# Three changes of order in a hybrid attention block: residual tiles turned back before the last one is turned forth, eight PSUM banks in the last down projection, outputs scaled ahead of the query products

## The reference

```python
def rms_norm(x, gain):
    y = xf * lax.rsqrt(jnp.mean(xf * xf, axis=-1, keepdims=True) + NORM_EPS) * gain
...
    # chunk_gated_delta_rule, one step a chunk
    def step(state, inp):
        v_new = u_i - w_i @ state
        o_i = q_i @ state + qk_i @ v_new
        state = state * gt_i + k_i.T @ v_new
...
    o = o * lax.rsqrt(jnp.mean(o * o, axis=-1, keepdims=True) + NORM_EPS) * head_norm * silu(z)
    y = sigmoid(g_a) * o + sigmoid(g_b) * multiscale_causal_pool(...)
    mixer = y @ w_out
...
    h = h + hybrid_mixer(rms_norm(h, norm_mix), ...)
    h = h + conv_gated_mlp(rms_norm(h, norm_ffn), w_up, conv_ffn, w_down)
    return rms_norm(h, norm_final)[:, N_META:]
```

## Time and profile before

| what | us |
| --- | --- |
| median of 3 runs (1780.7 to 1784.41) | 1781.15 |
| the profiled execution | 1779.33 |
| its span | 1777.5 |
| TensorE busy | 1692.4 |
| VectorE busy | 909.4 |
| ScalarE busy | 609.4 |
| GpSimd busy | 472.9 |
| mean granted clock of TensorE | 0.98 |

### The profile page before, as it was taken

One profiled execution on the slowest core, in us unless ns is written; L12 is line 12 of the kernel. 1 busy time (PEld: TensorE's weight loads), 2 busy tenths in 40 slices (PEclk: granted clock), 3 DMA queues, 4 the chain that ended last, 5 costly groups with the idle time before them and its releaser, 6 DMA issues.

```text
span 1777.5 us, 30704 instructions
## 1 busy us (share of the span) xinstructions
PE 1692.4 (95%) x12131; PEld 1616.4 (91%) x12131; DVE 909.4 (51%) x971; ACT 609.4 (34%) x984; POOL 472.9 (27%) x469
## 2 busy tenths in 40 slices
PE   6999999986999999999879999999999999999997
PEld 6999999986999999999879898989989989989986
DVE  5565644582445454454450656455455455455457
ACT  6334465443434444343322531211211212212213
POOL 3221212124343444434202121221221221221220
PEclk9999999997999999999979999999999999999998
DMA  5223443336353544545584111111111111111112
GB/s 187 75 91 109 135 131 92 110 88 185 110 151 100 156 107 136 151 119 142 132 257 150 36 36 36 59 47 35 59 47 35 58 42 42 47 47 47 47 35 95
DMA packets 239653, 167.41 MB, mean 94 GB/s; under 512 B 43880, under 2 KB 225991, under 8 KB 238456
## 3 DMA queue, kind: packets, MB, share of 16 engines
q1 hardware_dynamic: 205492, 130.39, 25.7%
q10 hardware_dynamic: 33892, 36.28, 6.0%
q0 software_dynamic: 224, 0.12, 0.0%
HBM read 124.40 MB, written 42.37 MB: 94 GB/s over the span
## 4 chain that ended last, share of the span: by engine, by line
PE 84%; DVE 7%; DMA 2%; ACT 2%; SPq 1%; issue 1%; DVEq 1%; ACTq 0%; POOL 0%; POOLq 0%
PE gb L787 60%; PE db L1115 13%; PE db L926 4%; DMA yb_d<-ybs 1%; PE db L840 1%; PE db L991 1%; DVEq L1550 1%; PE db L992 1%; SPq L583 1%; DMA yo<-ot_d 1%; DVE cacc L1587 1%; DVE tiny L1748 1%; DVE vb L1751 1%; DVE hx L1879 1%; PE db L1068 1%
## 5 line engine op out<-in xcount | busy, mean ns | idle before, releaser
L787 PE MATMUL gb<-u_hi,w_hi 128*128 128x342 f32 (+2 forms) x2520 | 824.3, 327 | 14.7 <-ACT ht L1459 5.1
L787 PE MATMUL gb<-u_lo,w_hi 128*128 128x342 f32 (+2 forms) x2520 | 811.5, 322 | 0.0
L787 PE MATMUL gb<-u_hi,w_lo 128*128 128x342 f32 (+2 forms) x2520 | 808.4, 321 | 0.0
L673 POOL TENSOR_TENSOR w_lo<-w_raw,w_hi 128x1024 fp32r<-128x1024 f32 x128 | 324.2, 2538 | 1089.9 <-ACT w_hi L1157 1089.9
L787 PEld LDWEIGHTS gb<-u_hi,w_hi 128*128 128x128 f32 x2520 | 478.9, 190 | 19.2 <-issue 16.2
L787 PEld LDWEIGHTS gb<-u_lo,w_hi 128*128 128x128 f32 x2520 | 478.8, 190 | 0.4
L787 PEld LDWEIGHTS gb<-u_hi,w_lo 128*128 128x128 f32 x2520 | 478.2, 190 | 0.0
L1951 DVE TENSOR_TENSOR h<-h,db 128x512 f32<-128x512 f32 x176 | 117.2, 685 | 59.0 <-PE db L1115 58.6
L1115 PE MATMUL db<-w_hi,a_hi 128*128 128x512 f32 x352 | 141.1, 401 | 2.9 <-DVE a_lo L1975 2.9
L1115 PE MATMUL db<-w_lo,a_hi 128*128 128x512 f32 x352 | 139.7, 397 | 0.0
L1115 PE MATMUL db<-w_hi,a_lo 128*128 128x512 f32 x352 | 139.7, 397 | 0.0
(11 more groups left out here) (234 smaller groups left out, 1691.2 us busy)
## 6 DMA issues: line engine op xcount, KB each, us to landing
w_raw<-in_w_in SPq DMA_DIRECT2D x53, 512.0 KB, 3.9
w_raw<-in_w_up SPq DMA_DIRECT2D x44, 512.0 KB, 3.8
w_raw<-in_w_down SPq DMA_DIRECT2D x22, 512.0 KB, 3.3
qkT_d<-sl ACTq DMA_DIRECT2D x16, 576.0 KB, 2.8
kv_d<-tm ACTq DMA_DIRECT2D x16, 576.0 KB, 3.4
tk<-kv_d SPq DMA_DIRECT2D x9, 1024.0 KB, 7.6
kT<-qkT_d SPq DMA_DIRECT2D x9, 512.0 KB, 4.8
qT<-qkT_d SPq DMA_DIRECT2D x9, 512.0 KB, 7.9
```

What stands on the lines that cost most here:

```text
L673: pool.tensor_tensor(w_lo[:, n % SLOTS, :], w_raw[:, n % SLOTS, :], w_hi[:, n % SLOTS, :].bitcast(F32), ALU.subtract).then_inc(s_wlo, 1)
L787: mm = pe.matmul(gb[:, bank, 0:w], wt, u, start=(k == 0 and m == 0), stop=(k == KT - 1 and m == 2))
```

## The change

1. `output_scale(c)` is called at the end of VectorE's part of SU instead of at the start of its part of OT, so ahead of the two `qkm` products of QK.
2. In `OUT_PLAN` "back" j + 2 stands ahead of "forth" j + 1. So that the other engines follow, VectorE's `low2(j)` and `scale2(j + 1)` are moved into "forth" j, and ScalarE's root of tile j + 1 too (`root2`); for tiles 0 and 1 both stay in "back".
3. In the last down projection the first three matmuls run ahead for u = 0 to 7. `down_bank` gives u % 8 = 4 to 6 the banks `gb` and 7 the bank `mb`. Ahead of u = 4 TensorE waits until ScalarE has emptied `gb`; a bank is now waited for eight outputs later, and VectorE adds from the same banks.

```diff
-OUT_PLAN += [("unit", 5, 1), ("back", 0), ("unit", 6, 1), ("forth", 0), ("back", 1)]
+OUT_PLAN += [("unit", 5, 1), ("back", 0), ("unit", 6, 1), ("back", 1), ("forth", 0)]
...
-    OUT_PLAN += [_unit, ("forth", _j + 1), ("back", _j + 2)]
+    OUT_PLAN += [_unit, ("back", _j + 2), ("forth", _j + 1)]
...
+        def down_bank(u, last=False):
+
+            if not last or u % 8 < 4:
+                return db[:, u % 4, :]
+            return gb[:, u % 4, :] if u % 4 < 3 else mb[:, :]
...
-            for u in range(4):
+            for u in range(KT):
+                if u == 4:
+                    pe.wait_ge(s_gfree, U_FFN + 12 * (FFN_ITERS - 1))
                 down_part(W_LAST, u, 0)
             for u in range(2 * KT):
                 if u % KT == 0:
                     pe.wait_ge(s_alo, FT + u // KT)
-                if u > 3:
-                    pe.wait_ge(s_dnfree, 16 * (FFN_ITERS - 1) + u - 3)
+                if u >= KT:
+                    pe.wait_ge(s_dnfree, 16 * (FFN_ITERS - 1) + u - KT + 1)
                     down_part(W_LAST, u, 0)
                 down_part(W_LAST, u, 1).then_inc(s_dn, 1)
...
+            def root2(j):
+                n = HALO if j == 0 else P
+                act.wait_ge(s_h2, 2 * j + 2)
+                if j >= 2:
+                    act.wait_ge(s_hnt, 2 * (j - 1))
+                root(j, n, h2m[:, :] if j == 0 else h2[:, j - 1, :], hx[0:n, j % 2, :], s_h2sq)
...
                 elif kind == "back":
...
+                    if tile[0] < 2:
+                        root2(tile[0])
                 else:
                     high2(tile[0])
+                    if 0 < tile[0] < KT:
+                        root2(tile[0] + 1)
...
                 elif name == "OT":
-                    output_scale(c)
                     dve.wait_ge(s_bd, 16 * (c + 1) + 16)
...
                     halves(name, c, lambda h: dve.tensor_tensor(heads(st, h), heads(st, h), dbank(name, h),
                                                                 ALU.add), s_ev[name])
+                    output_scale(c)
...
                 if kind == "back":
                     residual(tile[0])
-                    if tile[0]:
-                        low2(tile[0] - 1)
+                    if tile[0] < 2:
+                        scale2(tile[0])
                 elif kind == "forth":
-                    scale2(tile[0])
-            low2(KT)
+                    low2(tile[0])
+                    if 0 < tile[0] < KT:
+                        scale2(tile[0] + 1)
...
-                    dve.tensor_tensor(dst, dst, db[:, u % 4, :], ALU.add).then_inc(s_dnfree, 1)
+                    dve.tensor_tensor(dst, dst, down_bank(u, isinstance(i, int) and i == FFN_ITERS - 1), ALU.add).then_inc(s_dnfree, 1)
```

More of the change, by code:

```diff
@@ L1114, in down_part @@
                 for m, (a, wt) in enumerate(((a1, w1), (a1, w2), (a2, w1))):
-                    mm = pe.matmul(db[:, u % 4, :], a, wt, start=(q == 0 and m == 0), stop=(q == 1 and m == 2))
+                    mm = pe.matmul(down_bank(u, n == W_LAST), a, wt, start=(q == 0 and m == 0), stop=(q == 1 and m == 2))
                 return mm
@@ L1469, in _ @@
                 elif kind == "back":
-                    j = tile[0]
-                    n = HALO if j == 0 else P
-                    act.wait_ge(s_h2, 2 * j + 2)
-                    if j >= 2:
-                        act.wait_ge(s_hnt, 2 * (j - 1))
-                    root(j, n, h2m[:, :] if j == 0 else h2[:, j - 1, :], hx[0:n, j % 2, :], s_h2sq)
+                    if tile[0] < 2:
+                        root2(tile[0])
                 else:
                     high2(tile[0])
+                    if 0 < tile[0] < KT:
+                        root2(tile[0] + 1)
             def take(j, before, i=0):
```

## The result

The changed kernel takes 1759.12 us, median of four runs (1757.38 to 1760.06). The kernel before took 1780.98 us beside it (four runs, 1780.7 to 1784.41). The ratio is 0.9872, with a 95% interval of 0.9855 to 0.9889. The profiled execution took 1758.65 us, where that of before took 1779.33: 20.7 us less.

The account below looks back on a forecast made before the run. TensorE, busy 1692.4 of 1777.5 us, was taken as the bound, so only its idle or low-clock time could be won. Parts of 14.5 + 3.4 + 1.4 = 19.3 us off 1781.15 gave 1761.9, said as 1762; range 1757 to 1768.

Parts of the forecast that it names:

- three mechanisms: Mask holds VectorE's small scaling product; back first readies `hx` before forth; extra matmuls fill the gap ahead of `a_lo`.
- The room of X0: Recurrence, round 1: X0 has 5.3 us to spare before it waits for `rrs`, 3.8 left after the move.
- part 1, waits for `vb`: Recurrence: TensorE's waits for the scaled output vanish in seven rounds, the ninth chunk's stays; 17.4 - 4.6 = 12.8 us.
- part 1, clock in round 1: Recurrence, behind round 1's wait: granted clock 0.83 for 10 us, won back without idle time; 1.7 us, at least 0.
- part 2, waits for `hx`: Output projection's end: forth's waits for `hx` fall in all eight places, 8 x 0.34 = 2.7 us.
- part 2, the first unit's wait: Output projection's end: the first waiting "up" unit's wait falls from 2.26 to 1.62 us, 0.64 won.
- part 3: Last down projection: filling the 2.86 us gap at full clock ends the first two sums 1.4 us earlier, bounds 0 and 1.6.
- a few more rounds: Recurrence, upper bound: 1.7 us of clock for each further round with a low-clock stretch, in executions that have more.
- The rival that more clock comes back: Recurrence: two or three more rounds' worth of clock, 3 to 5 us, 1757 to 1759; inside the forecast's 0.82.
- The rival stood nearer: Recurrence: inverse comes late, X0 waits for `rrs` each round, 1791 at 9 us delay; chance 0.05, 0.03 of it slower.
- its count of eight rounds: Late-inverse rival: each us of delay beyond 5.3 costs 8 rounds a us, less the 19.3 won.
- Its deciding delay: Late-inverse rival: the kernel is slower than before once the inverse's delay passes 5.3 + 2.4 = 7.7 us.

Follow-up runs that it names:

- the later mask: Kernel before, scaling where it was, GpSimd's next mask made behind its products of the values and keys: 1769.68 us.
- the double mask: GpSimd's mask written twice with the same values: 1784.42 us in the kernel before, 1761.18 us in the changed kernel.
- part 1 alone: Kernel before with only the outputs scaled ahead of the query-key products: 1765.56 us.
- six memsets: Changed kernel with six GpSimd memsets of an unused scratch ahead of the inverse's signal in each round but the first: 1800.24 us.
- the filler: Kernel before with twelve dummy matmuls in TensorE's gap ahead of the wait for `a_lo`: 1781.69 us.
- back alone: Kernel before with only "back" put ahead of "forth", and the moves that go with it: 1775.96 us.
- the late table: Kernels without the early table load; the changed kernel with that load (dummy square root) and an earlier turn back took 1757.87 us.

## Why the prediction was right, and which terms were mis-sized

Forecast 1762, measured 1759.12, within the range; for the profiled execution 19.3 us against 20.7. The three mechanisms were right, and two terms of the sum were mis-sized, both by the idle column. The room of X0, which is no term of the sum, was put too high. The terms:

| term | forecast, us | measured, us |
|---|---|---|
| part 1, waits for `vb` | 12.8 | 14.6 |
| part 1, clock in round 1 | 1.7 | 1.5 |
| part 2, waits for `hx` | 2.7 | 4.1 |
| part 2, the first unit's wait | 0.64 | 0.64 |
| part 3 | 1.4 | 1.26 |

**Part 1, the mechanism: right.** The small product fell from 1.87 to 0.17 us, the scaling moved into VectorE's idle time, and `qkm` was not pushed back (it starts 4.36 us behind the start of the additions, as before). The run with the later mask shows that it was the mask, and the double mask that the hold goes by who starts first.

**Part 1, the size: 14.5 forecast, 16.2 measured.** The term that was too small is 17.4 - 4.6 = 12.8, summed from the idle column; it measured 14.6. That column counts from the modelled end of the last matmul, but consecutive matmuls overlap, so that the next could have started before this end. The right measure is from start to start. In the timeline of before, the last matmul ahead of the OT of 524.57:

```profile
522.39 0.32 PE L787 MATMUL gb<-u_hi,w_lo 128*128 128x342 f32 x1
```

And in that of after the same pair:

```profile
522.00 0.32 PE L793 MATMUL gb<-u_hi,w_lo 128*128 128x342 f32 x1
522.15 1.04 PE L929 MATMUL db<-cst,vb 128*128 128x128 f32 x8
```

From start to start that is 2.18 against 0.15: 2.03 us, and another 0.05 since the group itself takes 0.85 to the next matmul instead of 0.80. So each wait shown as 1.86 us costs 2.08. Even the last round of the earlier trace rows, which shows no idle time, has 0.40 us from start to start ahead of its OT and so costs 0.3. Six rounds of 2.08, round 0 with 1.85 and the last with 0.30 are 14.6; with the clock's 1.5 (below) that is 16.1, and the table of marks has 16.23. The later mask's rest of 0.4 us for a shown 0.16 is the same thing.

**The clock behind round 1: right, 1.7 forecast.** Round 1 took 56.01 us and the next 54.58 and 54.54: 1.5. The changed kernel's round 1 is 52.44. All five profiled executions that have these waits show the long round 1 (56.0 to 56.1), and none a second one; so the bound for "a few more rounds" was empty. The rival that more clock comes back gave 1757 to 1759 us, close to the measured 1759.12, but not by its reason: no execution has a second long round. What clock there is beyond the forecast's is 1.5 us in four executions of six, at the output projection's end, behind the wait of 2.26 us; more of the missing time, 1.8 us here and 1.4 in part 2, is the idle column's.

**What is late next: the reading held, the number did not.** The room of X0 was put at 5.3 us, 3.8 at the least. Measured it is 2.1 to 4.9 in one execution of the changed kernel, 2.9 to 4.9 in the other, and 2.1 to 3.1 with part 1 alone. I had allowed for the scaling holding GpSimd's small steps, by its own length, and one such hold is in the rows above. What I had not seen is that the inverse's start moves against the recurrence from round to round, with the DMA that brings `blk`; it was read in round 1 and the last alone. A late start and a hold come together, and so the room goes under the least that was allowed for. The rival stood nearer than I said, though its count of eight rounds was one too many, since round 0 did not wait even with six memsets. Its deciding delay was forecast as 7.7 us; with the mean room of 3.8 us and 1.5 us of clock behind each wait (9.0 + 1.4 over seven), 22 us are used up when 7 x (delay - 3.8 + 1.5) is 22, at some 5.4 us. That is an estimate; measured are two points, 8.2 us of mean delay with 17 us slower than before, and some 3 us of delay with 2 us given back.

**Part 2: 3.4 forecast, 4.8 measured, some 6 in most executions.** The waits of "forth" are gone in all eight places and the two units wait 1.62 each, as the steps said. Mis-sized is again the idle column: 0.34 shown is 0.66 from start to start against 0.16, and in the middle the period fell from 6.08 to 5.52 us. 8 x 0.34 = 2.7 was in truth 4.77 - 0.64 = 4.1, 0.5 each. The 0.64 held from start to start too, 2.53 less 1.89. The 1.5 us of clock behind the 2.26 us wait are not in any term, because the one execution that was read had none.

**Part 3: 1.4 forecast, 1.26 measured**, by the mechanism given (restart and clock), which the filler shows. It isn't the same in every execution. Of the five profiled ones that have the gap, three take 737.15 to 737.17 us from the last delayed unit to the last `fino`, the other two 736.90 (back alone) and 739.69 (later mask); without the gap it is 735.89 to 735.91 in all that have the late table. In the two odd ones the low clock comes after the restart, where TensorE's pace of 1.28 us for an output sets VectorE's additions, and costs 0.7 and 1.0 us between the first reciprocal and the last `fino`; the later mask's other 1.5 is a low stretch behind its last 1.62 us wait. The timeline of VectorE in the run with back alone:

```profile
1747.56 0.69 DVE L1963 TENSOR_TENSOR h<-h,db 128x512 f32<-128x512 f32 x1 [0.24 <-PE db L1121]
1748.84 0.69 DVE L1963 TENSOR_TENSOR h<-h,db 128x512 f32<-128x512 f32 x1 [0.59 <-PE db L1121]
1750.12 0.69 DVE L1963 TENSOR_TENSOR h<-h,db 128x512 f32<-128x512 f32 x1 [0.59 <-PE db L1121]
```

**The sum.** 16.23 + 4.77 + 1.26 - 0.11 = 22.15, less the 1.46 by which the changed kernel's execution came later into the recurrence: 20.7. So 19.3 lies as near to 20.7 as it does partly by luck; without that late start it would be 22.15, and what the sum left out is in the main the idle column's 3.2 us. The medians differ by 21.9.

## What to carry to other kernels

Price a wait of TensorE from the start of the last matmul to the start of the next, against the same pair where nothing is late; a column of idle time that begins at modelled ends leaves 0.2 us out of each wait, and hides the shortest whole. Ahead of a VectorE product with two SBUF inputs, look at what GpSimd starts in the same tenth of a microsecond: a product of 128x8 can cost 1.9 us. When a step is moved, measure the room of the next late thing in every round and in more than one execution, look at which DMA starts the chain in front of it, and add the clock to each wait that might come.

## What the runs showed of the hardware

The granted clock behind a wait differs with the wait and between executions of one kernel. Behind seven waits of 1.86 us in a row it fell once, in round 1, in all five executions. Behind the wait of 2.26 us it fell in four executions of six, behind the waits of 1.62 us once in nineteen. Behind each of the seven waits of 3.8 to 4.7 us, 1.3 to 2.0 us more than the wait were lost. Why round 1 alone is hit among equal waits stays open; no run here tells it.

GpSimd's memsets, which read nothing, were not held: two of 128x1024 took 2.03 us at 516.82 in the run with six of them, beside VectorE's product of 1.23 us at 516.60.
